# Keys and compressed keys/values turned by VectorE blocks and memory instead of TensorE, and a reordered start, in a transformer layer kernel

## The reference

```python
h = x
h = h + nsa_mixer(rms_norm(h, norm_mix_g), w_in, q_g, k_g, cmp_pos, cmp_w1, cmp_w2, w_out)
h = h + square(relu(rms_norm(h, norm_mlp_g) @ mlp_w1)) @ mlp_w2
h = h + sigmoid(rms_norm(h, ple_norm_g) @ ple_w_gate) * (p @ ple_w_proj)
# nsa_mixer(u): 16 heads of 128, 4 groups of keys and values
q, k_c, v_c, k_s, v_s, k_w, v_w, gate = split(u @ w_in)
def compress(t, pos, w1, w2):          # blocks of 32 tokens, stride 16: 15 of them
    ch = t.reshape(bsz, seq // 16, 16, G, dk)
    blk = concatenate([ch[:, :-1], ch[:, 1:]], axis=2) + pos[:, None, :]
    return silu(einsum('bnlgd,lde->bnge', blk, w1)) @ w2
k_c = rms_norm(compress(k_c, ...), k_g[0]);  v_c = compress(v_c, ...)
k_s = rms_norm(k_s, k_g[1]);  k_w = rms_norm(k_w, k_g[2])
o = gate0 * attend(q, k_c, v_c) + gate1 * attend(q, k_s, v_s) + gate2 * attend(q, k_w, v_w)
return o @ w_out
```

## Time and profile before

| what | value |
|---|---|
| median of 3 runs | 1208.03 us (1207.96 to 1209.53) |
| the profiled execution | 1209.89 us |
| its span, first to last instruction | 1207.8 us |
| TensorE busy | 1196.9 us (99%) |
| VectorE busy | 729.1 us (60%) |
| ScalarE busy | 590.7 us (49%) |
| GpSimd busy | 71.5 us (6%) |
| moved by DMA | 247.02 MB, 205 GB/s on average |

### The profile page before, as it was taken

One profiled execution on the slowest core, in us unless ns is written; L12 is line 12 of the kernel. 1 busy time (PEld: TensorE's weight loads), 2 busy tenths in 40 slices (PEclk: granted clock), 3 DMA queues, 4 the chain that ended last, 5 costly groups with the idle time before them and its releaser, 6 DMA issues.

```text
span 1207.8 us, 15258 instructions
## 1 busy us (share of the span) xinstructions
PE 1196.9 (99%) x5502; PEld 993.3 (82%) x5502; DVE 729.1 (60%) x956; ACT 590.7 (49%) x812; POOL 71.5 (6%) x63
## 2 busy tenths in 40 slices
PE   8999999999999999999999999999999999999998
PEld 7787788888888888888888888888888888888886
DVE  5676646777767647554465464555655457476554
ACT  6654444666656544443344443444433445455442
POOL 1000000000000002100011100011100012000000
PEclk9999999999999999999999999999999999999999
DMA  9776564333348766865567765577665676785661
GB/s 353 251 228 211 186 195 139 104 123 105 105 144 266 223 222 217 253 224 193 188 215 244 240 215 194 189 237 242 220 217 191 208 245 214 248 266 195 212 208 51
DMA packets 107134, 247.02 MB, mean 205 GB/s; under 512 B 9408, under 2 KB 52160, under 8 KB 107072
## 3 DMA queue, kind: packets, MB, share of 16 engines
q1 hardware_dynamic: 106784, 245.98, 62.4%
q10 hardware_dynamic: 288, 0.27, 0.1%
HBM read 232.58 MB, written 13.63 MB: 204 GB/s over the span
## 4 chain that ended last, share of the span: by engine, by line
PE 92%; DVE 3%; ACT 2%; DMA 2%; issue 1%; SPq 0%; ACTq 0%; DVEq 0%
PE acc L1413 85%; DMA w_raw<-in_nsa_w_in_units_dram 2%; PE sc L1554 2%; DVE w_split L936 1%; PE tr L1471 1%; ACT w_split L595 1%; ACT s L693 1%; PE sc L1519 0%; PE sc L1460 0%; PE tr L1460 0%; PE tr L1605 0%; PE tr L1606 0%; PE acc L1443 0%; ACT junk_act L645 0%; PE tr L1583 0%
## 5 line engine op out<-in xcount | busy, mean ns | idle before, releaser
L936 DVE TENSOR_TENSOR w_split<-w_raw,w_split 128x1024 fp32r<-128x1024 f32 x411 | 509.3, 1249 | 384.2 <-ACT w_split L595 383.7
L595 ACT ACTIVATE w_split<-w_raw 128x1024 fp32r<-128x1024 f32 x411 | 431.4, 1058 | 413.0 <-PE acc L1413 407.2
L1413 PE MATMUL acc<-w_split,a_hi 128*128 128x512 f32 x1916 | 595.5, 392 | 1.7 <-DVE w_split L936 1.7
L1413 PE MATMUL acc<-w_split,b_split 128*128 128x512 f32 x1920 | 441.0, 390 | 0.0
L1413 PEld LDWEIGHTS acc<-w_split,a_hi 128*128 128x128 f32 x1916 | 357.0, 188 | 77.0 <-DVE w_split L936 3.0
L1413 PEld LDWEIGHTS acc<-w_split,b_split 128*128 128x128 f32 x1920 | 359.3, 188 | 74.2
L1413 PE MATMUL acc<-w_split,a_lo 128*128 128x512 f32 x958 | 373.5, 390 | 0.0
L1413 PEld LDWEIGHTS acc<-w_split,a_lo 128*128 128x128 f32 x958 | 180.2, 188 | 38.0
L559 POOL TENSOR_TENSOR stage<-stage 128x512 f32<-128x512 f32 x32 | 49.8, 1577 | 558.8 <-ACT stage L603 558.8
L693 ACT ACTIVATE s<-s,nmx,q_scale 128x128 f32<-128x128 f32 (+1 forms) x64 | 34.2, 540 | 5.4 <-DVE nmx L1103 5.4
L603 ACT ACTIVATE stage<-acc,rstd 128x512 f32<-128x512 f32 x48 | 30.1, 678 | 11.3 <-PE acc L1413 8.2
(11 more groups left out here) (185 smaller groups left out, 516.3 us busy)
## 6 DMA issues: line engine op xcount, KB each, us to landing
w_raw<-in_mlp_w_units_dram SPq DMA_DIRECT2D x256, 512.0 KB, 4.3
w_raw<-in_nsa_w_in_units_dram SPq DMA_DIRECT2D x79, 512.0 KB, 4.3
w_raw<-in_nsa_w_out_units_dram SPq DMA_DIRECT2D x32, 512.0 KB, 3.8
w_raw<-in_ple_w_gate_units_dram SPq DMA_DIRECT2D x32, 512.0 KB, 3.6
turn_dram<-junk SPq DMA_DIRECT2D x44, 128.0 KB, 4.3
turn_dram<-s SPq DMA_DIRECT2D x44, 128.0 KB, 4.3
v_slc<-turn_dram SPq DMA_DIRECT2D x22, 256.0 KB, 4.4
v_win<-turn_dram SPq DMA_DIRECT2D x22, 256.0 KB, 4.2
```

The costliest lines, as they stand in the source:

```text
L595: nc.scalar.activation(w_hi[:, u % SPLIT], w_raw[:, u % RAW], ACT.Copy).then_inc(hi_done, 1)
L936: nc.vector.tensor_tensor(w_lo[:, u % SPLIT], w_raw[:, u % RAW], f32(w_hi[:, u % SPLIT]), ALU.subtract).then_inc(lo_done, 1)
L1413: last = nc.tensor.matmul(acc[c % 2][t][:], xs[:, kt, toks], ws[:, u % SPLIT, m * NW:(m + 1) * NW], start=(kt == 0 and n == 0), stop=(kt = ...
```

## The change

The first transfers: x tiles 0 and 1 (128 KB each) now go on SyncE's queue, each just ahead of its half of unit 0, no longer as one transfer on ScalarE's. `keep_busy` now does 10 matmuls of zeros from `causal`, whose memset is first on GpSimd. The sums of squares stand behind units 6, 7, 8 and 9, one column chunk each; rstd and the read-out of C_KC come one unit earlier. p is loaded and split in the last output chunks.

The four transpose sets on TensorE go. Their chunks are turned by `turn_blocks` behind units 12 (C_KC), 20 (C_VC), 32 (C_KS) and 44 (C_KW), SyncE sends them away at units 20, 28, 40 and 52 and back two units later, all through `s1` and `p_t`. `pos_part` for the keys moves from behind units 14, 15 to 18, 19; for the values from behind 22, 23 to behind 28, 29, after compress(0), and on ScalarE ahead of the read-out of C_KS. `keys_hi`/`keys_out` of k_s move to behind unit 42, of k_w to behind 53 and 54; TensorE waits for the last of it before the first head's scores.

```diff
+T_KC, T_VC, T_KS, T_KW = range(4)
+KEY_TURNS = {T_KC: FIRST[C_KS] + 4, T_VC: FIRST[C_KW], T_KS: FIRST[C_VS], T_KW: FIRST[C_VW] + 4}
...
+        early_blocks = s1[:].rearrange("p a b s -> p (a b s)")
+        early_turned = p_t[:].rearrange("p b s -> p (b s)")[:, 0:TT * NW]
...
             def turn_back(n, i=0):
 
+                if n in (T_VC, T_KS, T_KW):
+                    sp.wait_ge(turned_split, n)
                 sp.wait_ge(turn_out[n % 2], 16 * (P // QUAD) * (n // 2 + 1 + 2 * i))
...
                         for m, full in enumerate((first_full, raw_full[0])):
+                            sp.dma_start(x_raw[:, m], x_cols[:, m]).then_inc(first_x[m], 16)
                             sp.dma_start(slot(0)[:, m], packed(w_in_units, col // NW, 0)[:, m]).then_inc(full, 16)
...
+                    for n, away in KEY_TURNS.items():
+                        if u == away:
+                            turn_away(n)
+                        if u == away + 2:
+                            turn_back(n)
...
-                        sp.dma_start(p_raw, p_cols).then_inc(p_full, 16)
...
+            nc.gpsimd.memset(causal[:], 0.0).then_inc(busy_zeros, 1)
...
-            act.dma_start(x_raw[:, 0:UNIT_KT], x_cols[:, 0:UNIT_KT]).then_inc(x_cols_full[0], 16)
...
             def pos_part(kv, half):
 
                 if half:
-                    for b in range(2):
-                        act.wait_ge(tr_done[b], R_KC + kv + 1)
+                    act.wait_ge(turned_split, T_KC + kv + 1)
                 else:
                     act.wait_ge(pos_added, kv + 1)
...
+            def keys_hi(n, br):
+
+                act.wait_ge(turn_in[n % 2], 16 * TT * (n // 2 + 1))
+                for t in range(TT):
+                    last = nc.scalar.activation(k_hi[:, :, t, br].rearrange("p m (g j) -> p m g j", j=QUAD),
+                                                turned_tiles(n)[:, :, 4 * t:4 * t + 4], ACT.Copy,
+                                                scale=const_t[:, GAIN_K + 1 + br:GAIN_K + 2 + br])
+                last.then_inc(turned_hi, 1)
...
             for k in split_hi(FIRST[C_KC], UPC):
                 if k < UPC - 1:
                     x_part(k + 1)
+                if k >= 6:
+                    x_sums(k - 6)
             for k in split_hi(FIRST[C_VC], UPC):
                 if k < 2:
-                    for n in range(2 * k, 2 * k + 2):
-                        act.wait_ge(x_full[n], 16)
-                        sum_squares(0, n)
-                if k == 3:
+                    x_sums(k + 2)
+                if k == 2:
                     act.wait_ge(const_full, 16)
                     act.wait_ge(rs_ready, 1)
                     to_stage(C_KC, rstd[:, 0])
-                if k >= 6:
-                    pos_part(0, k - 6)
             for k in split_hi(FIRST[C_KS], UPC):
                 if k == 2:
-                    act.wait_ge(tr_full[1], R_KC + 1)
+                    act.wait_ge(blocks_turned, TT * (T_KC + 1))
                     to_stage(C_VC, rstd[:, 0])
-                if k >= 6:
-                    pos_part(1, k - 6)
+                if k in (2, 3):
+                    pos_part(0, k - 2)
             for k in split_hi(CMP_FIRST[0], CMP_UNITS):
                 pass
             for k in split_hi(FIRST[C_KW], UPC):
+                if k < 2:
+                    pos_part(1, k)
                 if k == 0:
-                    act.wait_ge(tr_full[1], R_VC + 1)
+                    act.wait_ge(blocks_turned, TT * (T_VC + 1))
                     to_stage(C_KS, rstd[:, 0])
...
+            def keys_turn(n):
+
+                dve.wait_ge(normed, n - T_KS + 1)
+                turn_blocks(n, lambda t: stage[:, t])
...
+            def keys_out(n, br):
+
+                dve.wait_ge(turned_hi, n - T_KS + 1)
+                for g in range(G):
+                    low = k_low(g // 2)[:, g % 2 * NW:(g % 2 + 1) * NW].rearrange("p (t b s) -> p t b s", t=TT, b=2)
+                    for t in range(TT):
+                        last = nc.vector.scalar_tensor_tensor(
...
             def pos_part(kv, half):
 
 
+                n = T_KC + kv
+                if not half:
+                    dve.wait_ge(turn_in[n % 2], 16 * TT * (n // 2 + 1))
+                col = POS + kv * CL + half * (CL // 2)
+                for g in range(G):
+                    last = nc.vector.tensor_tensor(
...
+                last.then_inc(turned_split if half else pos_added, 1)
                 dve.wait_ge(pos_hi, 2 * kv + half + 1)
...
             for k in split_lo(FIRST[C_VC], UPC):
...
+                if k == 4:
+                    for t in range(TT):
+                        dve.wait_ge(acc_read[C_KC % 2][t], C_KC // 2 + 1)
+                    turn_blocks(T_KC, lambda t: stage[:, t])
             for k in split_lo(FIRST[C_KS], UPC):
-                if k >= 6:
-                    pos_part(1, k - 6)
+                if k in (2, 3):
+                    pos_part(0, k - 2)
+                if k == 4:
+                    for t in range(TT):
+                        dve.wait_ge(acc_read[C_VC % 2][t], C_VC // 2 + 1)
+                    turn_blocks(T_VC, lambda t: stage[:, t])
...
             for k in split_lo(FIRST[C_KW], UPC):
-                if k == 1:
+                if k < 2:
+                    pos_part(1, k)
+                if k == 2:
                     staged_mean_square(1, C_KS)
                 if k == 2:
                     hidden_sum(0)
                 if k == 3:
                     staged_scale(1)
+                if k == 4:
+                    keys_turn(T_KS)
...
+                    if s == 8 and not g:
+                        pe.wait_ge(turned_split, T_KW + 1)
...
-                    nc.tensor.transpose(sc[1][:, 0:P], ident[:], ident[:])
-
+                    nc.tensor.matmul(sc[1][:, 0:P], causal[:, 0:P], causal[:, 0:P], start=True, stop=True)
+
+            pe.wait_ge(busy_zeros, 1)
+            keep_busy(10)
             pe.wait_ge(set_up, 2)
-            keep_busy(18)
...
-                if k == 4:
-                    staged(C_KC)
-                    transpose_set(R_KC, from_stage)
...
-                if k == 4:
-                    staged(C_VC)
-                    transpose_set(R_VC, from_stage)
...
-                if k == 5:
-                    pe.wait_ge(normed, 1)
-                    transpose_set(R_KS, from_stage)
...
-                if k == 5:
-                    pe.wait_ge(normed, 2)
-                    transpose_set(R_KW, from_stage)
```

More of the change, by code:

```diff
@@ L106 @@
 LATE_UNITS = 4
-R_KC, R_VC, R_KS, R_KW = range(4)
 def q_set(g):
-    return R_KW + 5 * g if g else R_KW + 1
+    return 5 * g - 1 if g else 0
 def p_set(h):
-    return R_KW + 1 + h + min((h + 1) // HPG + 1, G)
+    return h + min((h + 1) // HPG + 1, G)
 R_H1 = p_set(H - 1) + 1
@@ L127, in hi_sets @@
     if r >= R_H1:
-        return r - R_H1 + 3 + G
-    return r - R_KS + 1 if r <= R_KW else (r - R_KW) // 5 + 3
+        return r - R_H1 + 1 + G
+    return (r + 1) // 5 + 1
 R_H2 = R_H1 + 1
-T_H1 = 0
-T_HID = 3
+T_H1 = 4
+T_HID = T_H1 + 3
 T_H2 = T_HID + 4 * QUARTERS
@@ L179, in trunk_layer @@
         s0 = sb("s0", [P, 2, 2, P])
+        with nc.sbuf_tensor("p_raw", [P, 2, SEQ], F32) as p_raw, \
+                nc.sbuf_tensor("pt_hi", [P, 2, SEQ], F32R) as pt_hi, nc.sbuf_tensor("pt_lo", [P, 2, SEQ], F32R) as pt_lo:
+            pass
         p_t = sb("p_t", [P, 2, NW + SEQ])
         p_cmp = sb("p_cmp", [P, 2, SEQ], F32R)
-        kc_rows, kc_sq = (p_t[0:N_CMP, b, 0:NW] for b in range(2))
+        kc_rows, kc_sq = junk_act[0:N_CMP], junk[0:N_CMP, 0:NW]
         mx = sb("mx", [P, 2, 4])
@@ L222, in trunk_layer @@
         x_full = [sem(f"x_full{n}") for n in range(4)]
-        x_cols_full = [sem(f"x_cols_full{k}") for k in range(UPC)]
+        first_x = [sem(f"first_x{m}") for m in range(UNIT_KT)]
+        x_cols_full = [sem(f"x_cols_full{k}") for k in range(1, UPC)]
+        busy_zeros = sem("busy_zeros")
         x_hi = sem("x_hi")
@@ L289, in trunk_layer @@
         turn_dram = nc.dram_tensor("turn_dram", (4, P // QUAD, QUAD, P // QUAD, TT, P), F32, kind="Internal").ap()
-        blocks = (junk[:], s1[:].rearrange("p a b s -> p (a b s)"))
-        turned = [v[:].rearrange("p t n -> p (t n)") for v in (v_slc, v_win)]
+        early_blocks = s1[:].rearrange("p a b s -> p (a b s)")
+        early_turned = p_t[:].rearrange("p b s -> p (b s)")[:, 0:TT * NW]
+        late_blocks = (junk[:], early_blocks)
+        late_turned = [v[:].rearrange("p t n -> p (t n)") for v in (v_slc, v_win)]
         block = ctx.enter_context(nc.Block())
@@ L321, in hid_sum, with blocks, turned @@
             return v_win[0:2 * HID + 1, kv, 0:DK]
+        def blocks(n):
+            return early_blocks if n < T_H1 else late_blocks[n % 2]
+        def turned(n):
+            return early_turned if n < T_H1 else late_turned[n % 2]
         def turned_tiles(n):
-            return turned[n % 2].rearrange("p (g m j) -> p m g j", m=NW // P, j=QUAD)
```

(13 more changed lines are left out.)

100 lines of the change are left out of this document (44 added, 56 removed).

## The result

The changed kernel takes 1214.1 us at the median (1213.65 to 1217.72), the kernel before on the same chip 1208.03. The ratio is 1.0054, with a 95% interval of 1.0043 to 1.0065: 6 us slower where 2.9 had been forecast. The direction and the place were right, the size was not.

The account below looks back on a forecast made before the run. TensorE, busy 1196.9 of 1207.8 us, bounds the kernel. Start -1.1, unit 16 -0.4, transposes -3.5, late keys +0.2, stalls +6.8, C_VS +0.7 sum to +2.7; clock +0.2 gives +2.9: 1210.9, 8 in 10 within 1205.5 to 1214.5, own range 1209 to 1213.

Parts of the forecast that it names:

- The chain at units 29 to 31: After compress(0): serial adds, roundings, read-out and low halves on VectorE and ScalarE stall TensorE by 3.0, 2.25 and 1.6 us.
- C_VS: Units 42 to 44: eight small low-key instructions and the block transposes on VectorE cost +0.7, between 0 and 1.2.
- the 0.2 set aside for it: Clock falling to 0.50 behind the stalls; only what reaches beyond unit 31 counts: +0.2, at most 1.4.
- the fourth rival: Clock falls in the stalls and stays down behind unit 31: 1212.3, chance 0.10.
- The first two rivals: Units 29 to 31: chain fits, no stalls, 1203.7, chance 0.15; or only bare periods count, 4.3, about 1207.8, chance 0.29.
- the third: Turned values or keys come back 2 to 3 us later, memory shared with weights: 1213.5, chance 0.12.
- The start, -1.1: Start to unit 10: earlier first matmul and spread sums of squares gain 1.1 us, between -1.6 and 0.
- between no delay and 0.7 I take 0.2: Start: delay from SyncE's two more transfers, 0.45 us each, ahead of unit 1's, with one on ScalarE's queue gone.
- The bound that I gave the start, 0: Worst case of the start term: a slow clock into unit 1 costing 1.1 us cancels the gain.
- The stalls, +6.8: Units 29 to 31 behind compress(0): stalls of 3.0, 2.25 and 1.6 us; from below 4.3, from above 7.7.
- four of 256 with their overhead 1.45: Chain link at unit 29: VectorE's position adds as four of 256 take 1.45, against 1.28 for two of 512.
- The upper bound: Stalls at most 7.7: strided reads dearer than PSUM ones, +0.1 on each of eight adds, and values back late.

Follow-up runs that it names:

- turn_only: Changed kernel with the start of before (first transfers, fillers, sums of squares); all four sets turned by VectorE and memory: 1216.29, ratio 1.0053 to the kernel before.
- late_vpos: Changed kernel with the values' two position parts behind units 34 and 35 instead of 28 and 29: 1209.15, ratio 1.0003 to the kernel before.
- best2: Kernel before with sums spread, all four sets turned by VectorE and memory, values' position parts behind units 31 and 34, satisfied waits added: 1206.26, ratio 0.9980.
- xfer_only: Kernel before with sums of squares spread and x tiles 0 and 1 as two transfers in SyncE's queue, old fillers: 1207.27, ratio 0.9984.
- sums_only: Kernel before with sums of squares spread over units 6 to 9, first transfers and fillers as before: 1205.6, ratio 0.9973; run again 1206.08, 0.9978.
- start_only: Kernel before with the new start (transfers, fillers, spread sums), all transposes kept on TensorE: 1207.41, ratio 0.9988 to the kernel before.
- contig: Changed kernel with the four position adds reading turned data in the order it lies (wrong elements, same work): 1212.77, ratio 1.0042 to the kernel before.
- after_pad: Changed kernel with 16 tiny matmuls of zeros (64 instructions) behind the 10 start fillers: 1215.99, ratio 1.0073 to the kernel before.
- keys_only: Kernel before with only k_s and k_w turned by VectorE and memory, start and compressed part as before: 1212.37, ratio 1.0033.

## Why the prediction was right in direction and wrong in size

**Right.** Each transposed set costs TensorE 0.9 us: 0.92 between units 10 and 12, of which some 0.1 is the old wait at unit 10 that is gone, and 0.8 between units 31 and 42. The chain at units 29 to 31 has the links, the order and the releaser that were named, and it is the largest term. C_VS cost 0.8, nearly all of it by the small instructions of the low keys, the block transposes next to nothing. Turning k_s and k_w has no late reader. The clock did fall in the stalls, and it was back at 92.76, before unit 31, so that neither the 0.2 set aside for it nor the fourth rival's price was paid; behind other waits, in turn_only, late_vpos and best2, it was, with 1.5 to 1.7 each time. The first two rivals, that the chain would fit or half of it would, are refuted by these 8.0 us; the third showed itself only in turn_only.

**The start, -1.1, measured +0.1.** The step that failed is "between no delay and 0.7 I take 0.2". Two issues of 0.45 stand ahead of unit 1's weights, and these are issued at 3.14 instead of 2.19. The whole of that came through, and more: x's tiles for unit 7 were there at 24.56 instead of 23.30. From there the forecast's own chain holds: 24.56, 0.8 for x's tiles, sums 1.5, rounding 1.06 and low half 1.23, start at 29.34, and three more units to 37.6. The bound that I gave the start, 0, came out only by luck: it had been worked out from a slow clock, and the clock was at 1.00 here (a pair of matmuls takes 0.71 at 11.72). xfer_only and the two runs of sums_only show the two halves in their traces: spread sums -1.2 to -1.5 at unit 10, new transfers +1.0 to +1.2. How late the tiles are differs from trace to trace, 0.4 us in start_only's and 1.3 in the changed kernel's against the 23.30 before, and why is open.

**The stalls, +6.8, measured +8.0.** The step that failed is "four of 256 with their overhead 1.45". It was priced from a row in which the add reads the turned chunk out of PSUM. By its code that read has a stride too, of 16 elements, and it took 1.28 for the same elements in two instructions. The new one reads tiles in SBUF with strides of 16 and 128 elements, and takes 2.16 in four; in order, in contig, it is 1.42. So it was not the number of instructions but the strided read from SBUF, for which the forecast had no row. The upper bound had 0.1 for each of eight adds; it was 0.18. The direct delay is 1.4 (8.2 less contig's 6.8); the table has 1.2 because the kernel before loses 0.26 in these units as well.

These two, 1.2 each, are 2.4 of the 2.6 by which 2.7 missed 5.3. The rest of the 6.07 came from places that the prediction did not look at. TensorE's code after the change lies otherwise against the packets that bring it: 1.0 in the changed kernel's trace, set against after_pad's, and 3.6 in keys_only's. And the last units are 0.4 faster. How much the long jumps cost in the changed kernel's other executions is open. The measured 1214.1 lies inside the range for 8 in 10, 1205.5 to 1214.5, by 0.4, and outside the forecast's own, 1209 to 1213.

## What to carry to other kernels

Price a job by what stands behind it on its engine and by the lead at that place: the same two position parts cost 8 us behind compress(0), 3.5 behind units 34 and 35, 1.5 of that by a slow clock, and nothing in their old form and place. Turning data through VectorE and memory frees TensorE, but its reader then reads SBUF and not PSUM, and here a strided read of 128 x 256 from SBUF costs half as much again as one in order (1.42 to 2.16 for four), where the old strided read from PSUM did not show such a price (1.28 for the same elements). When an unrelated edit moves the time by microseconds far behind its place, compare the packets of the instruction queue and the durations of the loop's branch before looking for a cause in the data.

## What the runs showed that was not expected

- A loop of some 1616 TensorE instructions either fetches nothing on its second and third pass or all of it again (18 packets), depending on 34 instructions ahead of it. The same kernel took 1212.4 or 1208.4, 1.0033 or 0.9998 of the kernel before.
- The jump itself takes 3.3 to 3.8 us when it fetches. What TensorE loses by it differs: keys_only stood still for 1.30 and 1.65 us, some 14 instructions into the loop; the changed kernel for 0.19, over 40 in. Idle time understates it: by starts the two lost 3.6 and 1.0.
- A clock at 0.50 for 6.83 us cost the changed kernel nothing that can be seen, because the engine that fed TensorE was slower still. Where the next weights were ready, 3.41 us of it cost 1.5 to 1.7: unit 20 in turn_only, compress(1) in late_vpos, unit 32 in best2.
